# Two of the four sums of weight quarters in the last two feed-forward layers made by accumulating transfers

## The reference, cut to what matters

```
def swiglu(h, w_gate, w_up, w_down):
    return (jax.nn.silu(h @ w_gate) * (h @ w_up)) @ w_down
...
    h = swiglu(rms_norm(x, ff1_norm_pre[l]), ff1_w_gate[l], ff1_w_up[l], ff1_w_down[l])
    x = x + 0.5 * rms_norm(h, ff1_norm_post[l])
...
    h = swiglu(rms_norm(x, ff2_norm_pre[l]), ff2_w_gate[l], ff2_w_up[l], ff2_w_down[l])
    x = x + 0.5 * rms_norm(h, ff2_norm_post[l])
```

## Time and profile before

| | us |
|---|---|
| median of 3 runs (2280.52 to 2284.67) | 2283.95 |
| span of the profiled execution | 2280.9 |
| PE busy | 2245.4 (98%) |
| DVE busy | 1367.0 (60%) |
| ACT busy | 1072.6 (47%) |
| POOL busy | 737.0 (32%) |
| the paired loop of feed-forward 2 | about 1310.6 to 1493 |
| the paired loop of feed-forward 3 | about 1973 to 2155 |

### The profile page before, as it was taken

The page is one execution under the profiler, slowest core; times in us unless marked ns, Lnnn a source line. Parts: engine busy times, 40 slices in busy tenths (PEclk is TensorE's granted clock), DMA queues, the critical chain, the costliest instruction groups (busy, mean ns, idle before and its releaser), DMA issues.

```text
span 2280.9 us, 36680 instructions
## 1 busy us (share of the span) xinstructions
PE 2245.4 (98%) x13358; PEld 1934.1 (85%) x13358; DVE 1367.0 (60%) x1963; ACT 1072.6 (47%) x1850; POOL 737.0 (32%) x334
## 2 busy tenths in 40 slices
PE   8999999999999999999999999999999999999998
PEld 6668899988888887899988899988878768999987
DVE  7967666660453436666631899950557963899811
ACT  6665444442555554344432544441535665444512
POOL 6944422244322325321344311144111003311252
PEclk9999999999999999999999999999999999999999
DMA  6632332232211133223332233332422002323332
GB/s 211 197 93 94 110 107 98 99 101 96 80 65 66 64 103 120 96 98 101 102 100 85 93 102 110 95 106 95 149 82 75 29 11 83 107 98 109 101 102 93
DMA packets 64432, 223.79 MB, mean 98 GB/s; under 512 B 7120, under 2 KB 7120, under 8 KB 64336
## 3 DMA queue, kind: packets, MB, share of 16 engines
q1 hardware_dynamic: 60192, 208.30, 27.9%
q10 hardware_dynamic: 4144, 14.16, 2.0%
HBM read 211.88 MB, written 2.10 MB: 94 GB/s over the span
## 4 chain that ended last, share of the span: by engine, by line
PE 86%; DVE 5%; ACT 4%; issue 3%; DMA 1%; POOL 1%; DVEq 0%; SPq 0%; ACTq 0%; POOLq 0%
PE banks L645 9%; PE banks L678 9%; PE banks L680 9%; PE banks L679 9%; PE banks L646 9%; PE banks L647 9%; PE banks L859 5%; PE banks L860 5%; PE banks L861 5%; PE banks L906 3%; PE banks L905 3%; PE banks L904 3%; DVE banks L2603 2%; DMA raw<-ws 1%; PE banks L1257 1%
## 5 line engine op out<-in xcount | busy, mean ns | idle before, releaser
L563 POOL TENSOR_TENSOR wL<-raw,wH 128x1024 fp32r<-128x1024 f32 x194 | 497.6, 2570 | 756.9 <-ACT wH L1457 756.7
L1457 ACT ACTIVATE wH<-raw 128x1024 fp32r<-128x1024 f32 x371 | 391.9, 1058 | 680.8 <-PE banks L680 393.8
L645 PE MATMUL banks<-xH,wH 128*128 128x512 f32 (+1 forms) x1080 | 413.3, 383 | 11.2 <-DVE xL L2135 7.2
L646 PE MATMUL banks<-xL,wH 128*128 128x512 f32 (+1 forms) x1080 | 407.7, 377 | 0.0
L647 PE MATMUL banks<-xH,wL 128*128 128x512 f32 (+1 forms) x1080 | 407.5, 377 | 0.0
L678 PE MATMUL banks<-wH,hH 128*128 128x512 f32 x704 | 273.9, 389 | 0.0
L679 PE MATMUL banks<-wH,hL 128*128 128x512 f32 x704 | 273.9, 389 | 0.0
L680 PE MATMUL banks<-wL,hH 128*128 128x512 f32 x704 | 273.9, 389 | 0.0
L645 PEld LDWEIGHTS banks<-xH,wH 128*128 128x128 f32 x1080 | 203.6, 189 | 56.6 <-DVE wL L2140 7.9
L647 PEld LDWEIGHTS banks<-xH,wL 128*128 128x128 f32 x1080 | 203.6, 189 | 38.1
L646 PEld LDWEIGHTS banks<-xL,wH 128*128 128x128 f32 x1080 | 203.8, 189 | 35.1
(11 more groups left out here) (381 smaller groups left out, 5229.3 us busy)
## 6 DMA issues: line engine op xcount, KB each, us to landing
raw<-ws SPq DMA_DIRECT2D x371, 512.0 KB, 3.3
shifted<-gpad SPq DMA_DIRECT2D x32, 258.0 KB, 4.9
w1b<-w ACTq DMA_DIRECT2D x8, 512.0 KB, 5.6
tmp<-rows ACTq DMA_DIRECT2D x7, 512.0 KB, 3.8
b_row<-rows ACTq DMA_DIRECT2D x5, 512.0 KB, 3.8
tmp<-xT SPq DMA_DIRECT2D x8, 256.0 KB, 6.0
xr<-xN ACTq DMA_DIRECT2D x4, 512.0 KB, 3.7
out<-xr SPq DMA_DIRECT2D x3, 512.0 KB, 2.7
```

Source lines behind the costliest of these rows:

```text
L563: pool.tensor_tensor(wL[:, j, :], raw[:, j, :], fp(wH[:, j, :]), ALU.subtract).then_inc(low_ready, 1)
L645: pe.matmul(bank, wH[:, slot, cols], rh, start=start, stop=False)
L646: pe.matmul(bank, wH[:, slot, cols], rl, start=False, stop=False)
L1457: act.activation(wH[:, c % SLOTS, :], raw[:, c % SLOTS, :], ACT.Copy).then_inc(high_ready, 1)
```

## The change

- SP also loads the quarter a11 of each paired tile straight into the buffer of S1 (`load_part`, 256 KB), once product 4 of the tile two before has read that buffer; then the two chunks of the tile as before (`load_tile`).
- POOL issues two accumulating transfers for each paired tile (`add_parts`), both after it has waited for the load of the second chunk: one adds a22 onto a21 within the slot (SBUF to SBUF, 256 KB), the other adds the quarter a21, read again from `ws` in HBM, onto a11 in the buffer of S1 (256 KB).
- DVE loses the sums S1 and a21 + a22. What is left, S2 and S3 (`two_sums`), waits for the first accumulation (`w_added`). `first_two` went, and `two_sums` stands where `last_two` stood.
- ACT waits for `w_added` before the high part of slot s1, and for `part_added` before that of S1.
- POOL's order: the transfers of tile k + 1 are issued before the low part of S3 of tile k.
- The semaphores of the rows are merged from twelve to two, waited for by count in the order of the loads.

```
-        row_loaded = {n: sem(f"row_{n}") for n in ROWS}
+        gain_row_loaded = sem("gain_row_loaded")
+        shift_row_loaded = sem("shift_row_loaded")
...
+            def load_part(inst, t, j):
+
+                c = CHUNK[f"gateup{inst}"] + 2 * SEVEN_FROM[inst] + 2 * j
+                sp_e.wait_ge(product_done, t * 10 + (5 * seven_at(inst, j) - 6))
+                sp_e.dma_start(mixed_parts(j, MIX_S1)[2], ws[bass.ds(t * SLOTS + c, 1), :, 0:S].rearrange("o p n -> (o p) n"))\
+                    .then_inc(part_loaded[j], 16)
+
+            def load_tile(inst, t, j):
+
+                c = CHUNK[f"gateup{inst}"] + 2 * SEVEN_FROM[inst] + 2 * j
+                load_part(inst, t, j)
+                for i in (c, c + 1):
+                    sp_e.wait_ge(chunk_done, t * SLOTS + (i - SLOTS + 1))
+                    sp_e.dma_start(raw[:, i % SLOTS, :], ws[bass.ds(t * SLOTS + i, 1)].rearrange("o p n -> (o p) n"))\
+                        .then_inc(raw_loaded[i % SLOTS], 16)
...
+            def add_parts(inst, j, t):
+
+                c = CHUNK[f"gateup{inst}"] + 2 * SEVEN_FROM[inst] + 2 * (j % 2)
+                s, i, n = (c + 1) % SLOTS, j % 2, t + j // 2
+                pool.wait_ge(raw_loaded[s], n * 16 + 16 * ((c + 1) // SLOTS + 1))
+                pool.sem_inc(parts_begun, 1)
+                pool.dma_start(raw[:, s, 0:S], raw[:, s, S:2 * S], accum_op=ALU.add).then_inc(w_added[i], 16)
+                pool.wait_ge(part_loaded[i], n * 16 + (8 * paired_before(inst) + 16))
+                pool.sem_inc(parts_begun, 1)
+                pool.dma_start(mixed_parts(i, MIX_S1)[2],
+                               ws[bass.ds(n * SLOTS + (c + 1), 1), :, 0:S].rearrange("o p n -> (o p) n"),
+                               accum_op=ALU.add).then_inc(part_added[i], 16)
...
+                    add_parts(inst, 0, 0)
+                    add_parts(inst, 1, 0)
                     low_of_last_sum(u, 0, 0)
                     with pool.Fori(0, SEVENS[inst] - 1) as t:
+                        add_parts(inst, 2, t)
                         low_of_last_sum(u, 1, t)
+                        add_parts(inst, 3, t)
                         low_of_last_sum(u, 2, t)
...
                     high(c, t)
-                    act.wait_ge(w_mixed, t * 8 + (4 * (u + j) + 2))
+                    act.wait_ge(w_added[m], of_parity)
                     high(c + 1, t)
-                    act.wait_ge(w_mixed, t * 8 + (4 * (u + j) + 3))
-                    for n, made in ((MIX_S2, 3), (MIX_S1, 1), (MIX_S3, 4)):
+                    act.wait_ge(w_mixed, t * 4 + (mixes_before(inst) + 2 * j + 1))
+                    for n in (MIX_S2, MIX_S1, MIX_S3):
+                        if n == MIX_S1:
+                            act.wait_ge(part_added[m], of_parity)
...
-                    def first_two():
-                        for s, i in ((s0, c), (s1, c + 1)):
-                            dve.wait_ge(raw_loaded[s], t * 16 + 16 * (i // SLOTS + 1))
-                        dve.tensor_tensor(parts[MIX_S1][2], a11, a21, ALU.add).then_inc(w_mixed, 1)
+                    def two_sums():
+                        dve.wait_ge(raw_loaded[s0], t * 16 + 16 * (c // SLOTS + 1))
+                        dve.wait_ge(w_added[j % 2], t * 16 + (8 * paired_before(inst) + 16 * (j // 2) + 16))
+                        dve.tensor_tensor(parts[MIX_S2][2], a21, a11, ALU.add).then_inc(w_mixed, 1)
                         made(1)
-                        dve.tensor_tensor(a21, a21, a22, ALU.add).then_inc(w_mixed, 1)
-
-                    def last_two():
-                        made(2)
-                        dve.tensor_tensor(parts[MIX_S2][2], a21, a11, ALU.add).then_inc(w_mixed, 1)
-                        made(3)
                         dve.tensor_tensor(parts[MIX_S3][2], parts[MIX_S2][2], a12, ALU.add).then_inc(w_mixed, 1)
```

More of the change, by code:

```diff
@@ L340, in build_block @@
         w_mixed = sem("w_mixed")
+        w_added = [sem(f"w_added{j}") for j in range(2)]
+        parts_begun = sem("parts_begun")
+        part_loaded = [sem(f"part_loaded{j}") for j in range(2)]
+        part_added = [sem(f"part_added{j}") for j in range(2)]
         w_mix_high = sem("w_mix_high")
@@ L479, in seven_banks, with paired_before, mixes_before @@
             return (2, 3, 0, 1) if j == 0 else (6, 7, 4, 5)
+        def paired_before(inst):
+            return seven_at(inst, 0) - seven_at(2, 0)
+        def mixes_before(inst):
+            return 4 * seven_at(2, 0) + 2 * paired_before(inst)
         def mixed_parts(j, n):
@@ L496, in whole_h, with row_there @@
             return hW[:, bass.ds(f, 1), :].rearrange("p o t -> p (o t)")
+        GAIN_ROWS = ["mix_g0", "ffn_g0", "mix_g1", "ffn_g1", "ff1_post", "mix_post", "ff2_post"]
+        SHIFT_ROWS = ["pw2_b", "mix_b0", "ffn_b0", "mix_b1", "ffn_b1"]
+        def row_there(engine, name):
+            if name in GAIN_ROWS:
+                engine.wait_ge(gain_row_loaded, 16 * GAIN_ROWS.index(name) + 16)
+            else:
+                engine.wait_ge(shift_row_loaded, 16 * SHIFT_ROWS.index(name) + 16)
         block = ctx.enter_context(nc.Block())
@@ L542, in _, with loads @@
             load(c // SLOTS, c % SLOTS + 1)
[L543 to L547, removed]
+            def loads(lo, hi):
+                up, down = -(-lo // SLOTS) * SLOTS, hi // SLOTS * SLOTS
+                if up >= down:
+                    for c in range(lo, hi):
+                        load(c // SLOTS, c % SLOTS)
+                    return
+                for c in range(lo, up):
+                    load(c // SLOTS, c % SLOTS)
+                with sp_e.Fori(up // SLOTS, down // SLOTS) as t:
+                    for j in range(SLOTS):
+                        load(t, j)
+                for c in range(down, hi):
+                    load(c // SLOTS, c % SLOTS)
+            def load_part(inst, t, j):
[10 more added lines that the diff above has]
+                        .then_inc(raw_loaded[i % SLOTS], 16)
+            begun = SLOTS + 2 * KT
+            for inst in (2, 3):
+                cp = CHUNK[f"gateup{inst}"] + 2 * SEVEN_FROM[inst]
+                loads(begun, cp + 2)
+                load_part(inst, 0, 0)
+                loads(cp + 2, cp + SLOTS)
+                load_part(inst, 0, 1)
+                with sp_e.Fori(1, SEVENS[inst]) as t:
+                    for j in range(2):
+                        load_tile(inst, t, j)
+                begun = CHUNK[f"down{inst}"]
+            loads(begun, NCHUNKS)
             for q in range(QT - 1):
@@ L1522, in load_row @@
             def load_row(name, to):
-                act.dma_start(to, rows[ROWS.index(name)]).then_inc(row_loaded[name], 16)
+                loaded = gain_row_loaded if name in GAIN_ROWS else shift_row_loaded
+                act.dma_start(to, rows[ROWS.index(name)]).then_inc(loaded, 16)
             steps = [0]
@@ L2391, in low_slot @@
                         if n == 0:
-                            made(4)
+                            made(2)
                         s = (s0, s1)[n]
@@ L2521, in paired_h @@
                     if not last:
-                        last_two()
+                        two_sums()
                         low_slot(0)
@@ L2616, in _ @@
             dve.wait_ge(xN_loaded, 16 * QT)
-            dve.wait_ge(row_loaded["pw2_b"], 16)
+            row_there(dve, "pw2_b")
             for q in range(QT):
@@ L2620, in _ @@
             dve.wait_ge(res_step, QT)
-            dve.wait_ge(row_loaded["mix_g0"], 16)
+            row_there(dve, "mix_g0")
             for q in range(QT):
@@ L2626, in _ @@
                 low_tiles("mix0", h, 0, 4, shift="mix_b0")
-            dve.wait_ge(row_loaded["mix_b0"], 16)
+            row_there(dve, "mix_b0")
             ple(0)
             ffn(0, "mix0")
-            dve.wait_ge(row_loaded["ffn_g0"], 16)
-            dve.wait_ge(row_loaded["ffn_b0"], 16)
+            row_there(dve, "ffn_g0")
+            row_there(dve, "ffn_b0")
             for q in range(QT):
@@ L2696, in _ @@
                 low_tiles("mix1", h, 0, 4, shift="mix_b1")
-            dve.wait_ge(row_loaded["mix_b1"], 16)
+            row_there(dve, "mix_b1")
             ple(1)
             ffn(1, "mix1")
-            dve.wait_ge(row_loaded["ffn_g1"], 16)
-            dve.wait_ge(row_loaded["ffn_b1"], 16)
+            row_there(dve, "ffn_g1")
+            row_there(dve, "ffn_b1")
             add_block("down1", 0)
```

23 lines of the change are left out of this document (11 added, 12 removed).

## The result

The changed kernel takes 2359.45 us (median of 4 runs, 2358.29 to 2360.9) against 2282.98 for the kernel before on the same chip. The ratio is 1.0335 with a 95% interval of 1.032 to 1.0349. The profiled execution took 2360.9 with a span of 2359.0, which is 78.1 more than the span before; the medians differ by 76.5. I had said 2385.

The account below looks back on a forecast made before the run. PE bounds the kernel, and a closed loop through the load sets the changed tile: span 2280.9 + 100.6 (34 tiles x 2.96) + 0.6 for first tiles = 2382.1, with 3.05 from span to median 2385 us; range 2320 to 2455.

Parts of the forecast that it names:

- What bounds it: In the two paired-tile loops PE is the bound, busy 159.95 of 160.00 us; relieving DVE wins under 2 us together.
- the break-even: The change costs nothing if the time from the load's landing to the accumulated quarter's release is 1.54 us.
- the closed loop through the load: Load, accumulation, S2 and product 7 follow each other; the next load is issued only then, so added latency lengthens each tile.
- 8.59 + x: New length in us of a paired tile, x being the time from the load's landing to the accumulated quarter's release; 10.13 before.
- T + 3.91: When DVE sees the load landed in a paired tile: 3.91 us after T, the start of the tile's product 1.
- x = 4.5: Load landing to accumulated quarter's release: 3.3 us movement plus about 1.2 for POOL and the second transfer; tile 13.09 us.
- The short transfer of the rivals: Accumulation in the loops released after only 2.7 us: tile 11.3 us, 39 us lost, 2323; case 2300 to 2358, chance 0.18.
- The forecast with its chance of 0.50: Main case: the accumulated quarter is released 3.7 to 5.3 us after the load's landing, giving 2358 to 2413.
- The upper end of my range: 2455 us, for the accumulated quarter released 6.6 us after the load's landing; the range leaves out some 2 in 10.
- The first tile: First tile of each loop: nearly free, its sums beginning 7.16 us before its first matmul; about 0.3 us per loop.
- POOL's queue, ACT, SP: In the loops POOL's later low part of S3, ACT's wait for the accumulation and SP's added load are hidden, costing nothing.
- The clock rival: PE's idle piece ahead of product 7 halves its pace in each tile: 1.44 us more, 49 in all, 2434; chance 0.07.

Follow-up runs that it names:

- the first experiment: The changed kernel, but DVE makes a21 + a22 again and only the sum S1 comes from POOL's accumulating transfer: 2343.03 us, ratio 1.0263.

## Why the prediction was right in its account and 26 us too high

**What bounds it, and the break-even: right.** PE had no time to give, and the closed loop through the load is what sets the tile. The experiment with the sum ahead of S2 cuts this loop at product 7, and most of the loss goes.

**8.59 + x: right.** From S2 to product 7 there are 3.16 us (3.15 in the prediction). By the prediction's own measure, x runs from T + 3.91 to S2, here from 1403.42 to 1407.13, which is 3.71. 8.59 + 3.71 = 12.30, and the tile has 12.31.

**x = 4.5: the step that failed.** It was the one term without a row, taken between 3.3 and 4.9. It is 3.71: 3.35 from POOL's start to DVE's, as I had put the movement alone, and 0.36 for POOL ahead of it (1403.42 to 1403.78) instead of the 1.2 that I added. The second transfer beside it didn't stretch it: without that one the median landing is 3.3 us too. 34 tiles x (12.30 - 10.13) = 73.8 instead of 100.6. The short transfer of the rivals, x = 2.7, is what a plain copy by POOL comes to (0.36 + 2.3); adding to the target costs 1.0 us more than overwriting it.

**How near it was.** The forecast with its chance of 0.50 began at 2358, from x = 3.7. The measured 2359.45 lies at that very edge, and by luck on the right side of it: without the 3.4 us of the clock (below) it would have come under the short transfer. Of the 26 us, 23.1 are in the span (2382.1 against 2359.0). The other 2.6 come from the offset between span and median: I had put it at 3.05 from the median of three runs and the span of one execution, and it is 0.45 here. The upper end of my range, from x = 6.6, should read 2457 and not 2455.

"DMA: Bandwidth & Descriptors" of the Trainium skill (Anatomy of one DMA) would have given an estimated 2.6 for the transfer. The plain copies come near it (2.3). The accumulating one took 3.3, so here the measurement decides.

**The first tile: right that it is nearly free.** Its first matmul comes 10.61 us after DVE's last sum of the full tile before it (L2444, 1302.58 to 1313.19), exactly as before (L2364, 1299.95 to 1310.56). It was put at 0.3 and is 0.

**POOL's queue, ACT, SP: hidden, as said.** Product 6 waited for POOL 0.2 us at most. I had asked only whether POOL's low part comes too late for PE. I hadn't asked what runs on DVE at its new time. In the change nothing does, so this cost nothing; in the first experiment the same move cost 51 us.

**The clock rival: in some tiles.** I gave it 0.07 for all tiles. Two tiles of the second loop have it. This stretch is one, with its granted clock of 0.75, and the first matmul of its product 7 follows:

```profile
2035.00:2039.00 4.00, 2.03 (x9) 2.03 (x10) 3.88 (x7) 1.70 (x4) 0.00 (x0) 0.75 0.31 122
```

```profile
2036.97 0.57 PE L934 MATMUL banks<-mixXH,wH 128*128 128x256 f32 x1 [2.56 <-DVE hW L2597]
```

It took 0.57 us instead of 0.39, and those behind it came every 0.21 instead of 0.12. Measured between POOL's transfers, the tiles took 13.12 and 14.85 us, together some 3.4 above the others. PE had been idle 2.56 us before it, against 1.6 in most tiles. With this, 73.8 + 3.4 = 77.2, near the 76.3 of the loops.

**Outside the loops: a small surprise.** The first loop begins 2.63 us later than before. That comes from the program's first matmuls. Before, a short break there (0.70 us from one matmul to the next, at 9.45) was soon followed by full pace. After, PE waited longer for a low part of DVE, and half pace lasted five us more:

```profile
10.99 0.80 PE L720 MATMUL banks<-xH,wH 128*128 128x512 f32 x1 [0.62 <-DVE wL L2220]
...
15.43 0.63 PE L721 MATMUL banks<-xL,wH 128*128 128x512 f32 x1
...
17.01 0.39 PE L720 MATMUL banks<-xH,wH 128*128 128x512 f32 x1
```

The kernel that only changes the order of before has the same wait of 0.6 us and a stretch at half pace until 14.5 too, and some kernels with the change have less: with the sum first, a wait of 0.46 us and full pace from 12.5. So it isn't tied to the change; why the break is longer in some programs stays open. 0.85 us come back between the loops: 76.3 + 2.6 - 0.8 = 78.1. One execution of each kernel was profiled, that of the change the slowest of its four. The medians differ by 76.5 us, which is no more than the loops lost, so these 1.8 us outside them may belong to this execution alone.

## What to carry to other kernels

A transfer that takes work off an engine is paid by its latency wherever its result closes a loop. Count from the landing of its input to the release of its reader before counting the instructions that it saves. Then look at what is queued behind that reader: two thirds of the loss here came from one sum that needed nothing of the transfer. And when work on GpSimd moves in time, ask what VectorE does at its new time, not only who waits for it.

## What the runs showed of the hardware that I had not expected

- An accumulating transfer of 256 KB inside SBUF took 3.3 us from issue to landing, a plain one 2.3. One that ran beside a load of 512 KB and another accumulation took 6.4.
- POOL started a transfer 0.5 to 0.6 us after the landing that it had waited for, SP about 0.02 us after.
- A DVE addition of 128x512 took 2.18 us instead of 0.69 when POOL's subtraction of the same shape (1.60 us) ran beside it, and 0.68 when that was moved away. In six such pairs, in six kernels, DVE's instruction ended 0.54 to 0.56 us behind POOL's, whatever its own length became (1.15 to 2.52 us), also where its record began 0.35 us before POOL's.
- The granted clock was 0.95 in two kernels and 1.00 in the change over the same stretch, though PE was idle for no longer in them. It was 0.75 where the accumulation was doubled.
